# First block of a two-block transformer: weights split into fp32r parts in the mixer and cross-attention, modulation weights folded by GpSimd

## The reference

```python
h = hybrid_mixer(x, ...)            # three branches, gates, w_mix_out
x = layer_norm(alpha * x + h, ...)
h = memory_cross_attention(x, mem, xa_q, xa_kv, xa_o)
x = layer_norm(alpha * x + h, ...)
h = conv_ffn(x, ffn_w_in, ffn_conv_w, ffn_conv_b, ffn_w_out)
x = layer_norm(alpha * x + h, ...)
```

## Time and profile before

| | |
|---|---|
| Median of 3 runs | 3057.61 us (3053.53 to 3058.78) |
| The profiled execution: its own time, its span | 3057.82 us, 3056.0 us |
| PE busy | 2977.3 us, 97% |
| PE weight loads busy | 2681.8 us, 88% |
| DVE busy | 1673.9 us, 55% |
| ACT busy | 1395.0 us, 46% |
| POOL busy | 418.5 us, 14% |
| DMA, mean | 222 GB/s |
| Mean granted TensorE clock | 0.979 |

### The profile page before, as it was taken

How to read it: one execution, slowest core, us unless ns; L and a number is a source line. 1 busy time by engine, 2 the same in 40 slices (tenths; PEclk the granted TensorE clock), 3 DMA queues, 4 the chain that set the end, 5 groups by cost and what they waited for, 6 DMA issues and landing times.

```text
span 3056.0 us, 39019 instructions
## 1 busy us (share of the span) xinstructions
PE 2977.3 (97%) x16790; PEld 2681.8 (88%) x16805; DVE 1673.9 (55%) x1839; ACT 1395.0 (46%) x1609; POOL 418.5 (14%) x164
## 2 busy tenths in 40 slices
PE   8999999999999999999999999999999999999997
PEld 6888888998788888998889998888988889988886
DVE  2465223663555222664534444267778778787784
ACT  2564012342464112443223342167767676676773
POOL 1000000001000000000000000023433343343332
PEclk9999999999999999999999999989999999999998
DMA  9675623546575633544235554269999999999993
GB/s 300 210 244 170 202 83 111 192 160 195 187 235 191 213 98 100 176 166 142 83 111 186 187 176 129 73 231 359 344 352 358 337 355 346 351 357 340 351 352 132
DMA packets 392050, 678.84 MB, mean 222 GB/s; under 512 B 17184, under 2 KB 286528, under 8 KB 391744
## 3 DMA queue, kind: packets, MB, share of 16 engines
q1 hardware_dynamic: 389344, 666.82, 63.1%
q0 software_dynamic: 2528, 9.46, 1.1%
HBM read 675.19 MB, written 4.69 MB: 222 GB/s over the span
## 4 chain that ended last, share of the span: by engine, by line
PE 94%; DVE 3%; ACT 1%; issue 1%; DMA 0%; SPq 0%; POOL 0%; DVEq 0%
PE bank L500 92%; PE bank L581 1%; PE bank L1046 1%; PE bank L604 0%; DVE ka L1293 0%; ACT w_hi L1700 0%; ACT x_hi L1718 0%; DVE work L1267 0%; DMA const<-in_const 0%; DVE xT L1377 0%; ACT gates L1708 0%; DVE w_lo L1196 0%; DVE ring_tail L1257 0%; DVE work L1152 0%; DVE ew_lo L1606 0%
## 5 line engine op out<-in xcount | busy, mean ns | idle before, releaser
L1606 DVE TENSOR_TENSOR ew_lo<-ring_head,ew_hi 128x1792 fp32r<-128x1792 f32 (+1 forms) x288 | 680.8, 2397 | 199.2 <-ACT ew_hi L1922 199.2
L1922 ACT CAST ew_hi<-ring_head 128x1792 fp32r<-128x1792 f32 (+2 forms) x384 | 647.8, 1696 | 274.0 <-PE bank L500 274.0
L482 POOL TENSOR_TENSOR ew_lo<-ring_head,ew_hi 128x1792 fp32r<-128x1792 f32 (+1 forms) x96 | 389.6, 4058 | 1195.7 <-ACT ew_hi L1922 1195.7
L1196 DVE TENSOR_TENSOR w_lo<-ring_head,w_hi 128x2048 fp32r<-128x2048 f32 x108 | 247.6, 2292 | 227.0 <-ACT w_hi L1700 227.0
L1700 ACT CAST w_hi<-ring_head 128x2048 fp32r<-128x2048 f32 x108 | 205.2, 1903 | 300.5 <-PE bank L500 255.8
L500 PE MATMUL bank<-x_hi,w_hi 128*128 128x256 f32 x1152 | 321.1, 284 | 0.5 <-ACT x_hi L1718 0.3
L500 PE MATMUL bank<-x_hi,w_lo 128*128 128x256 f32 x1152 | 318.6, 283 | 0.0
L500 PE MATMUL bank<-x_lo,w_hi 128*128 128x256 f32 x1152 | 318.5, 283 | 0.0
L500 PE MATMUL bank<-xT,ring_head 128*128 128x256 f32 x1408 | 312.2, 381 | 1.7 <-issue 1.7
L500 PEld LDWEIGHTS bank<-xT,ring_head 128*128 128x128 f32 x1408 | 267.5, 191 | 39.3 <-issue 3.3
L500 PE MATMUL bank<-ew_hi,xe_hi 128*128 128x448 f32 x1024 | 295.0, 369 | 4.4 <-DVE ew_lo L1606 4.4
(11 more groups left out here) (337 smaller groups left out, 4376.9 us busy)
## 6 DMA issues: line engine op xcount, KB each, us to landing
ring_head<-in_moe_w_gate SPq DMA_DIRECT2D x128, 896.0 KB, 6.6
ring_head<-in_moe_w_up SPq DMA_DIRECT2D x128, 896.0 KB, 6.9
ring_head<-in_moe_w_down SPq DMA_DIRECT2D x96, 1024.0 KB, 7.0
ring_head<-in_w_in SPq DMA_DIRECT2D x58, 1024.0 KB, 7.5
ring_head<-in_ffn_w_in SPq DMA_DIRECT2D x44, 1024.0 KB, 7.7
ring_head<-in_ada_w SPq DMA_DIRECT2D x30, 1024.0 KB, 5.3
ring_tail<-in_w_in SPq DMA_DIRECT2D x24, 1024.0 KB, 8.4
ring_head<-in_ffn_w_out SPq DMA_DIRECT2D x22, 1024.0 KB, 6.1
```

The lines of the kernel that those rows point to most:

```text
L482: pool.tensor_tensor(ew_lo[:, h, 0:n], ring(c % 6)[:, 0:n], ew_hi[:, h, 0:n].bitcast(F32), ALU.subtract).then_inc(w_used[c % 6], 1)
L1196: v.tensor_tensor(w_lo[:, h, :], ring(s), w_hi[:, h, :].bitcast(F32), ALU.subtract).then_inc(w_used[s], 1)
L1606: v.tensor_tensor(ew_lo[:, h, 0:n], ring(c % 6)[:, 0:n], ew_hi[:, h, 0:n].bitcast(F32), ALU.subtract).then_inc(w_used[c % 6], 1)
L1922: a.copy(ew_hi[:, c % DEPTH_HI, 0:n], ring(c % 6)[:, 0:n]).then_inc(f.count(part_hi), 1)
```

## The change

**Split weights in the first block.** Every one of the 62 chunks of a layer is now done by `three`: 48 fp32r matmuls (24 for a half chunk) in place of 16 (8) fp32 ones. ACT makes the high part in `high_part`, DVE the low part in `low_part`, which overwrites the chunk in its ring slot (`ring_low` is the same memory as `ring_head`). The ring has four slots here (4, 3, 1, 0); slots 5 and 2 and a third buffer hold the high parts. The six half chunks 31, 33, ... 41 of the branch products get their low part from POOL. The activations are split too: xs_hi and xs_lo, which with the third high buffer lie over `ring_tail`; and pairs for the branch outputs, the merged sum, the memory and the attention output. The sixth chunk uses bank 4 in place of bank 1.

**Modulation by GpSimd.** The ada_w chunks are loaded, scaled and added by POOL alone during the feed-forward part of each layer, in the three slots of `ring_tail`. POOL starts after the mean of the norm that precedes the feed-forward part. Results lie in `gates`, `merged` and `kb`. PE waits for all 24 (`folded`) after the last down products, and does the one-column matmuls in three places: 12 chunks around the end of the feed-forward part (in place of products of zeros), 12 in the head of the next layer or before the second block's first norm.

The core of the diff:

```diff
+CHUNKS = 62
+SLOT_OF = (4, 3, 1, 0)
+BY_POOL = (31, 33, 35, 37, 39, 41)
...
+        highs = [chunk_high[:, :], ring_low[:, 5, :], ring_low[:, 2, :]]
...
+                if s in held:
+                    sp.wait_ge(chunk_done, held.pop(s))
+                if s >= 6 and folds[0]:
+                    sp.wait_ge(folded, folds[0])
...
-                        load(kpn(w_in[l])[:, :, c * CW:(c + 1) * CW])
-                        load(kpn(io["ada_w_2"][l])[:, :, k * CW:(k + 1) * CW], None, ada_loaded)
...
+                    for i, (w, c) in enumerate(parts):
+                        load(kpn(w)[:, :, c * CW:(c + 1) * CW], SLOT_OF[i % 4])
```

POOL:

```diff
+                    for i in BY_POOL:
+                        n, at = (4 if 30 <= i < 42 else 8) * CW, SLOT_OF[i % 4]
+                        pool.wait_ge(chunk_hi, CHUNKS * l + i + 1)
+                        pool.tensor_tensor(ring_low[:, at, 0:n], ring(at)[:, 0:n], highs[i % 3][:, 0:n].bitcast(F32), ALU.subtract).then_inc(pool_lo, 1)
+
+                    def fetch(c):
+
+                        pool.dma_start(tiles(ring_tail[:, c % 3, :], KD), kpn(io["ada_w_2"][l])[:, :, c * CW:(c + 1) * CW]).then_inc(ada_loaded[c % 3], 16)
+
+                    pool.wait_ge(cond_ready, 1)
+                    pool.wait_ge(mean_ready, f.now(mean_ready) + 2)
+                    f.bump(mean_ready, 3)
+                    for c in range(3):
+                        fetch(c)
+                    for c in range(24):
+                        w = tiles(ring_tail[:, c % 3, :], KD)
+                        pool.wait_ge(ada_loaded[c % 3], f.next(ada_loaded[c % 3], 16))
+                        pool.tensor_tensor(w, w, cond[:, :].rearrange("p (k o) -> p k o", o=1).broadcast_to([P, KD, CW]), ALU.mult).then_inc(f.count(fold_step), 1)
+                        pool.wait_ge(fold_step, f.now(fold_step))
+                        pool.tensor_tensor(w[:, 0:4, :], w[:, 0:4, :], w[:, 4:8, :], ALU.add).then_inc(f.count(fold_step), 1)
+                        pool.wait_ge(fold_step, f.now(fold_step))
+                        pool.tensor_tensor(w[:, 0:2, :], w[:, 0:2, :], w[:, 2:4, :], ALU.add).then_inc(f.count(fold_step), 1)
+                        pool.wait_ge(fold_step, f.now(fold_step))
+                        pool.tensor_tensor(fold(c), w[:, 0, :], w[:, 1, :], ALU.add).then_inc(f.count(folded), 1)
+                        if c + 3 < 24:
+                            pool.wait_ge(folded, f.now(folded))
+                            fetch(c + 3)
```

PE:

```diff
+            def three(b, i, x, k=KD, turned=False, order=None, before=None):
+
+                pe.wait_ge(pool_lo if i in BY_POOL else chunk_lo, lows(l, i))
+                open_bank(b)
+                at = SLOT_OF[i % 4]
+                wh, wl = tiles(highs[i % 3][:, 0:k * CW], k), tiles(ring_low[:, at, 0:k * CW], k)
+                order = order or [(p, t, j) for j in range(2) for t in range(k) for p in range(3)]
...
                     ffn(FF1 // CW, FFN1_TRIP)
+                    pe.wait_ge(folded, 24 * (l + 1))
+                    modulation(0, range(12, 17))
                     for q in range(4):
                         pe.wait_ge(summed, f.next(summed))
                         mean_piece(q, 3)
-                    norm_var()
+                    modulation(0, range(17, 21))
+                    norm_var(idle=(0, 8), rest=lambda: modulation(0, range(21, 24), mods_full))
```

DVE and ACT:

```diff
+            def low_part(l, i):
+
+                n, at = (4 if 30 <= i < 42 else 8) * CW, SLOT_OF[i % 4]
+                if i not in BY_POOL:
+                    dve.wait_ge(chunk_hi, CHUNKS * l + i + 1)
+                    v.tensor_tensor(ring_low[:, at, 0:n], ring(at)[:, 0:n], highs[i % 3][:, 0:n].bitcast(F32), ALU.subtract).then_inc(chunk_lo, 1)
...
+                            if br == 0 and n:
+                                mix_low(n - 1)
+                            low_part(l, 33 + c)
+                    mix_low(3)
...
+                    if l + 1 < DEPTH:
+                        low_part(l + 1, 0)
+                        low_part(l + 1, 1)
...
+            def high_part(l, i):
+
+                n, at = (4 if 30 <= i < 42 else 8) * CW, SLOT_OF[i % 4]
+                loads[at] += 16
+                eng.wait_ge(w_loaded[at], loads[at])
+                if i >= 3:
+                    eng.wait_ge(chunk_done, CHUNKS * l + i - 2)
+                elif l:
+
+                    eng.wait_ge(*((folded, 24 * l), (down_done, 10 * l), (ffn_summed, 4 * l - 3))[i])
+                a.copy(highs[i % 3][:, 0:n], ring(at)[:, 0:n]).then_inc(chunk_hi, 1)
...
+                    high_part(l, 60)
+                    take(7, vb[:, :, CW:2 * CW])
+                    out_high(2)
```

More of the change, by code:

```diff
@@ L38, with lows @@
 NEG = -1.0e30
+CHUNKS = 62
+SLOT_OF = (4, 3, 1, 0)
+BY_POOL = (31, 33, 35, 37, 39, 41)
+def lows(l, i):
+    by_pool = sum(c <= i for c in BY_POOL)
+    if i in BY_POOL:
+        return len(BY_POOL) * l + by_pool
+    return (CHUNKS - len(BY_POOL)) * l + i + 1 - by_pool
 class Follow:
@@ L110 @@
+LAYERS = (LAYER1, LAYER1B)
 FFN1_TRIP = {
@@ L549, in tokens @@
                 spent.append(s)
[L551 to L555, removed]
-                open_bank(b)
-                for j in range(2):
-                    mm(bank[b][:, j:j + 1], w[:, 0, j * P:(j + 1) * P], one, True, True, bank_full[b] if j else None)
-                spent.append(ada_slot(c))
+            pieces_in = {x_hi_ready.name: 0, x_lo_ready.name: 0}
@@ new lines, in passes, with three_normed, before @@
+            def passes(ts, ps=(0, 1, 2)):
+                return [(p, t, j) for p in ps for t in ts for j in range(2)]
+            def three_normed(b, i):
+                def before(p, t, j):
+                    ready = (x_hi_ready, x_lo_ready, None)[p]
+                    if ready is not None and t % 2 == 0 and j == 0:
+                        pe.wait_ge(ready, pieces_of(ready))
+                three(b, i, xs, order=passes(range(KD), (0,)) + passes(range(6), (2,)) + passes(range(KD), (1,)) + passes((6, 7), (2,)),
+                      before=before)
@@ L561, in taken, with modulation @@
+            def modulation(at, chunks, full=None):
+                for c in chunks:
+                    for j in range(2):
+                        ins = nc.tensor.matmul(bank[at][:, 2 * (c % 12) + j:2 * (c % 12) + j + 1], fold(c)[:, j * P:(j + 1) * P], one,
+                                               start=True, stop=True)
+                if full is not None:
+                    ins.then_inc(mods_full, 1)
             def taken(b):
@@ L671, in _ @@
             norm_var()
-            pe.wait_ge(cond_ready, f.next(cond_ready))
             for l in range(DEPTH):
-                with f.trip(LAYER1):
+                with f.trip(LAYERS[l]):
                     turn[0] = 0
+                    if l:
+                        pe.wait_ge(mods_taken, 2 * l - 1)
                     for c in range(6):
-                        if c in (4, 5):
-                            tokens(c % 4, xT)
+                        if c == 5 and l:
+                            modulation(5, range(12), mods_full)
+                        if c == 0:
+                            three_normed(0, 0)
                         else:
-                            features(c % 4, xT, normed=c == 0)
+                            three(4 if c == 5 else c % 4, c, xs, turned=c in (4, 5))
                         if c == 4:
@@ L712, in _ @@
                             fill(u)
-                        else:
-                            modulation(2, 0)
+                        if u == 1 and l:
+                            pe.wait_ge(mods_taken, 2 * l)
                         if 1 <= u <= 16:
@@ L1700, in split_high, with kept, norm @@
                 a.copy(w_hi[:, h, :], ring(s)).then_inc(f.count(hi_ready[h]), 1)
-            def norm(eps, src, before, each=True, at=(4, 6)):
+            loads = [0] * 6
+            def high_part(l, i):
[7 more added lines that the diff above has]
+                a.copy(highs[i % 3][:, 0:n], ring(at)[:, 0:n]).then_inc(chunk_hi, 1)
+            def kept(biases):
+                for k in range(KD):
+                    ins = a.activation(xT[:, k, :], yT[:, k, :], ACT.Identity, bias=biases[:, k:k + 1])
+                ins.then_inc(f.count(x_ready), 1)
+            def norm(eps, src, before, each=True, at=(4, 6), covered=(None, None)):
                 a.preload_act_table(ACT.Sqrt)
@@ L1814, in _ @@
-                    biased(xT, par[:, A_LNB:A_LNB + 8], x_pieces, x_ready)
+                    for k in range(12, 15):
+                        sigmoid(k)
+                    for c in range(12):
+                        high_part(l, 33 + c)
+                        if c < 9:
+                            sigmoid(15 + c)
+                        if c % 3 == 2:
+                            part = slice(2 * (c // 3), 2 * (c // 3) + 2)
+                            eng.wait_ge(src_ready, f.next(src_ready))
```

(2 more changed lines are left out.)

404 lines of the change are left out of this document (273 added, 131 removed), and 21 rows, old and new, of tables (LAYER1, LAYER1B).

## The result

The changed kernel takes 3127.1 us (median of 4, 3119.39 to 3129.94), the kernel before beside it 3057.2. The ratio is 1.0226, 95% interval [1.0206, 1.0247]: slower by 70 us, where 3144 (a loss of 86) was forecast. The profiled execution took 3129.9 us, its span is 3128.2.

What follows compares the result with a forecast made beforehand. TensorE's matrix products were taken as the bound. From 3057.8 us, -153 (products -127.8, old modulation -17.2, old waits -32, new work +18.6 and -1.5, modulation elsewhere +6.8) and +239 for waiting on the folding gave 3144, range 3090 to 3185.

Steps and rivals of the forecast that it cites:

- Part 1: First block, both layers: three fp32r products in place of fp32 ones save 127.8 us.
- Parts 2 and 3: Attention stage: old modulation matmuls -17.2 us, old waits -32; new ACT and DVE work behind chunks +18.6, first norm -1.5.
- (a): After the last attention values: PE waits 1.9 us a layer while DVE copies a head and makes qa_lo.
- (c): Before the last value products: ACT's `take` stands behind high part 60, a wait of 2.7 us in place of 0.7.
- (b): Seam to w_mix: loads and low parts come late, waits of 4.9 us a layer in place of 1.5.
- (d): Branch products, where POOL makes half of the low parts: 2 us of waits a layer.
- The -32: Attention stage, two layers: PE's waits for DVE's adds and rotary products go, with slow spells behind them; 32 us saved.
- Part 5: Feed-forward part: POOL folds for 245 us a layer, plus 71 from exclusion with DVE; done 316 us after the mean.
- Part 6: Feed-forward end: PE waits 111 us a layer for `folded`, +222; work behind it +8.6, slow products +8; +239 us.
- no exclusion: Feed-forward part: POOL and DVE don't really exclude each other; 3002 us, faster; chance 0.18, half exclusion included.
- hidden wholly: Feed-forward part: folding takes 205 us or less and hides behind PE; 2912 us; chance 0.03.
- the mixer doesn't gain: Mixer: low parts, loads and DVE's reciprocals hold PE back at every third chunk; 3207 us; chance 0.16.

Runs made afterwards that it cites:

- no_fold: The changed kernel without GpSimd's loads and sums of the modulation weights (vectors are zeros): 3950 us, with the expert part running twice.
- all_dve: The changed kernel with the six low parts a layer that GpSimd makes in the branch products given to DVE: 3127.0 us, 1.0235.
- act_scale_start: act_scale with chunk 0's cast and subtraction at the kernel's start moved behind the first norm's scaling: 3004.5 us, 0.984.
- write_only: The changed kernel with memsets in place of GpSimd's product and sums, behind the same loads: no whole time given; second block starts at 1297.31 us.
- small_ops: The changed kernel with GpSimd's product in four instructions of 512 elements and the first sum in two: 3151.9 us, 1.036.
- act_scale: The changed kernel with ScalarE making the modulation product in eight pieces a chunk, GpSimd keeping sums and loads: 3011.3 us, 0.9855.

## Why the prediction was nearly right in time and wrong in place

**Part 1, products.** Without folding the whole first block gained 127.8 us (no_fold), where parts 1 to 4 and the tails of part 6 make -153 + 8.6 = -144.4: 17 us short. The attention window agrees with part 1: PE is busy 197.3 of 204.9 us at a clock of 0.99, for what took 269.

**Parts 2 and 3, waits.** Where rows named a wait, its size was good: (a) 1.7 a layer for 1.9, (c) 2.4 for 2.7, (b) a longest of 3.1, on `xs_lo`, for 4.9, (d) no wait at all for 2.0, and no loss without POOL's help (all_dve). What was short were waits that I did not list. DVE's copy of `va` holds PE 5.4 and 4.6 us, where it held it 0.8 each, and at the start `std` holds it 8.8, as the first norm stands behind a cast that waits for the first load; act_scale_start moved that cast and got 3.6 back. The first chunk starts at 34.0 us in place of 26.4. The 8.4 and the 7.6 are 16 of the 17 us. The -32 took for granted that nothing would come where the old waits went.

**Part 5, the folding.** It ends 300 and 301 us after the mean, forecast 316. The product is 3.60 us, not 4.6, so repeating `cond` made it cheaper and not dearer; the sums (2.34, 1.26, 0.72) are 0.3 us above the 4.0 of 1792 elements. Undisturbed, a chunk is 8.1 us with most of its waits, 9.6 from load to load; with the start near 236 a layer. The disturbance is then 64 us, forecast 71. The mutual exclusion was right, and right for the reason given: write_only shows that it hangs on POOL's reads.

**Part 6, what waits: this is the step that failed.** "PE itself loses some ... 30 a layer, which lies inside the 111 and costs nothing more." The 30 a layer was the term mis-sized. PE loses 60 us a layer to `w_lo`, 9.5 more to `x_lo` in layer 1, and 23 there by the clock, 17 of it behind the long waits. It is ready for `folded` at about 297 and 282 us, not at 205, and the 111 of idle time at the end are 2.4 and 19.3. The time comes near because POOL's end, forecast at 316 us and found at 300, is still the longer of two nearly equal paths: 203 us of cost for the +222 and +8 that part 6 gives to waiting and to the slow products behind it (its other 8.6 is counted above). That the second path did not pass the first is luck, as the prediction had it 80 us shorter than POOL's. And it costs by itself: take half of the folding away, so that POOL's end is far from mattering, and 83 of the 203 us stay. At that rate, 3.5 us a chunk, all 48 chunks make 167; the waits at the end are 22 more; some 14 stay open. The sentence "if PE's idle there is under 70 us, step 5 is wrong and so is the sign" was false on both counts: the idle time was 2.4 and 19.3, step 5 held, and so did the sign.

The sum by what was measured: 3057.8 - 127.8 + 203.1 - 3.1 (behind the second block's start) = 3130.0, against 3129.9 of the profiled execution. This only books what the starts of the second block give; it is no test.

Of the rivals, *no exclusion* is refuted by every pair of rows above, *hidden wholly* too; *the mixer doesn't gain* holds for 17 us of its 63.

## What to carry to other kernels

When a helper's work is stretched by excluding another engine, price both sides of the exclusion: not only when the helper ends, but what the held engine feeds. Here the second was nearly as long as the first, and shortening one made the other decide (small_ops). And then move the work to an engine that does not take part: ScalarE stood idle for 72% of the part, and with a load a slot earlier so that its queue waits 22.5 us for loads in place of 54.9, the same change is 2.1% faster than before in place of 2.3% slower. The second block still starts 56 us later than with nothing folded (1352.9 and 1297.0), with GpSimd's sums, ScalarE's pieces and their loads left. Untested is the split with the modulation left in the attention stage.

## What the runs showed of the hardware

- A GpSimd product over 2048 elements whose second operand is a column repeated 256 times takes 3.60 us; the plain sum over 1024 takes 2.34, over 512 1.26, over 256 0.72.
- GpSimd's product was hardly ever held up (median 3.62 us of 48, 3.60 alone), the sum that follows it nearly always (4.32 us or more in 20 of layer 1's 24, 2.34 alone). In the rows above one `w_lo` began at 490.81 and took 6.41 us, though POOL's next product began only at 491.44, behind the issue of a load, and took its usual 3.62. Why DVE came second there stays open.
- A DVE copy of eight elements, 0.17 us alone, took 2.22 in the mean beside GpSimd's reads and 0.73 beside its writes.
- TensorE's granted clock fell to its lower level behind a wait of 4.45 us (act_scale) and behind each of ten waits of 5.15 to 6.90 us in layer 1's feed-forward part, and stayed there for 2.7 to 5.7 us, 4.0 in the mean: about 1.7 us on top of each. Behind waits of 1.6 us or less for `w_lo` in that part it did not fall.
